# Conditioning tiles of two merges: multiplied and summed on VectorE instead of on TensorE

## The reference: what is computed

```
mc = split(silu(c_ctx) @ w_ada + b_ada, 6)      # context: shift1, scale1, gate1, shift2, scale2, gate2
ml = split(silu(c)     @ w_ada + b_ada, 6)      # latent tokens
merged = sigmoid(g0) * (y_ssd @ w_ssd_out) + sigmoid(g1) * (o_attn @ w_attn_out) + sigmoid(g2) * (o_pool @ w_pool_out)
x = x + gate1 * (merged @ w_out)
x = x + gate2 * moe(rms_norm(x) * (1 + scale2) + shift2)
```

## Time and profile before

| | |
|---|---|
| median of 3 runs | 2200.2 us (2199.82 to 2204.6) |
| the profiled execution | 2198.22 us, its span 2195.4 us |
| TensorE busy | 2054.4 us, 94% |
| VectorE busy | 1247.5 us, 57% |
| ScalarE busy | 956.9 us, 44% |
| DMA | 461.06 MB, 210 GB/s mean |
| conditioning matmuls, whole kernel | 134.4 us busy |

### The profile page before, as it was taken

How to read it: one execution, slowest core, us unless ns; L and a number is a source line. 1 busy time by engine, 2 the same in 40 slices (tenths; PEclk the granted TensorE clock), 3 DMA queues, 4 the chain that set the end, 5 groups by cost and what they waited for, 6 DMA issues and landing times. The chain is left out here.

```text
span 2195.4 us, 28102 instructions
## 1 busy us (share of the span) xinstructions
PE 2054.4 (94%) x11162; PEld 1732.8 (79%) x11162; DVE 1247.5 (57%) x1787; ACT 956.9 (44%) x1372; POOL 7.8 (0%) x12
## 2 busy tenths in 40 slices
PE   7899999989999999999999969987999999999994
PEld 2399988967888899999999958877777777777773
DVE  1467675426554333335433333365779879879996
ACT  1333564322443322223222233343667667667772
POOL 0000000000000000000000000000000000000000
PEclk9999999999999999999999989997999999999997
DMA  9944333333334555553455456532889889899991
GB/s 369 377 125 147 113 123 120 116 132 132 129 129 144 192 191 181 193 214 116 155 192 192 190 185 236 210 116 108 308 307 341 277 306 342 275 307 343 327 365 75
DMA packets 133521, 461.06 MB, mean 210 GB/s; under 512 B 17568, under 2 KB 23520, under 8 KB 133248
## 3 DMA queue, kind: packets, MB, share of 16 engines
q1 hardware_dynamic: 133376, 459.12, 58.8%
HBM read 455.06 MB, written 4.00 MB: 209 GB/s over the span
## 5 line engine op out<-in xcount | busy, mean ns | idle before, releaser
L180 DVE TENSOR_TENSOR wlo<-raw,whi 128x1024 fp32r<-128x1024 f32 x640 | 780.2, 1224 | 752.4 <-ACT whi L174 732.6
L174 ACT ACTIVATE whi<-raw 128x1024 fp32r<-128x1024 f32 x640 | 678.5, 1060 | 900.4 <-PE bank L202 446.3
L200 PE MATMUL bank<-hhi,whi 128*128 128x384 f32 x1664 | 569.0, 342 | 8.8 <-DVE wlo L180 3.6
L202 PE MATMUL bank<-hhi,wlo 128*128 128x384 f32 x1664 | 558.7, 336 | 0.0
L201 PE MATMUL bank<-hlo,whi 128*128 128x384 f32 x1664 | 558.5, 336 | 0.0
L200 PEld LDWEIGHTS bank<-hhi,whi 128*128 128x128 f32 x1664 | 314.0, 189 | 39.1 <-issue 24.1
L201 PEld LDWEIGHTS bank<-hlo,whi 128*128 128x128 f32 x1664 | 314.0, 189 | 0.8
L202 PEld LDWEIGHTS bank<-hhi,wlo 128*128 128x128 f32 x1664 | 313.8, 189 | 0.0
L2062 PE MATMUL bank<-whi,group_hi 128*128 128x512 f32 x512 | 203.1, 397 | 4.9 <-DVE wlo L180 3.7
L2064 PE MATMUL bank<-wlo,group_hi 128*128 128x512 f32 x512 | 201.6, 394 | 0.0
L2063 PE MATMUL bank<-whi,group_lo 128*128 128x512 f32 x512 | 201.0, 393 | 0.0
(11 more groups left out here) (309 smaller groups left out, 1983.9 us busy)
## 6 DMA issues: line engine op xcount, KB each, us to landing
raw<-in_dense SPq DMA_DIRECT2D x448, 512.0 KB, 5.4
raw<-in_moe SPq DMA_DIRECT2D x384, 512.0 KB, 5.0
merged<-in_x SPq DMA_DIRECT2D x8, 768.0 KB, 7.5
cs_rows_bc<-cs_rows SPq DMA_DIRECT2D x8, 768.0 KB, 5.1
out_y<-y_normed SPq DMA_DIRECT2D x3, 768.0 KB, 3.3
shift_rows<-cs_rows SPq DMA_DIRECT2D x2, 1024.0 KB, 9.2
pool_w_sb<-in_pool_w SPq DMA_DIRECT2D x1, 1024.0 KB, 6.9
pool_inv_count<-in_pool_inv SPq DMA_DIRECT2D x1, 768.0 KB, 4.9
```

What stands on the lines that cost most here:

```text
L174: self.nc.scalar.activation(self.whi[:, k % W, :], self.raw[:, n % R, :], ACT.Copy).then_inc(self.hi_done, 1)
L180: self.nc.vector.tensor_tensor(self.wlo[:, k % W, :], self.raw[:, n % R, :], self.whi[:, k % W, :].bitcast(F32), ALU.subtract).then_inc(se ...
L200: self.nc.tensor.matmul(out, self.whi[:, s, c], xhi[:, k, :], start=(k == 0), stop=False)
L202: last = self.nc.tensor.matmul(out, self.wlo[:, s, c], xhi[:, k, :], start=False, stop=(k == blocks - 1))
```

## The change

In the second and third merge TensorE no longer multiplies the conditioning tiles. VectorE does, from the same buffers in `raw`: for each half tile of 512 columns and for each of the two vectors one operation `parts` = `raw` x scalar + `parts` (a TENSOR_SCALAR without the addition for the first half tile of a chunk), the scalar being one value per partition from `cond_padded`. These are 4 operations a tile and 32 a chunk. In each turn 2 stand at A, 3 at B and 3 at C, behind the split and the merge there (`PART_STEPS`). The buffer of a conditioning tile is released when its four operations have ended (`load` waits for `s_part`, named `cond_part_added`). `parts` is double, by chunk. TensorE adds the sums over the partitions with 8 matmuls of one column a chunk, with `parts` as weights (`part_fold`). The copy of rows on ScalarE goes. The first stage, the first merge and the output projection are as before.

```diff
--- before.py
+++ after.py
@@ -103,6 +103,8 @@
         self.dve_steps = Steps(None, nc.alloc_semaphore("dve_steps"))
         self.used = nc.alloc_semaphore("tile_used")
         self.ada_used = nc.alloc_semaphore("cond_tile_used")
+        self.s_part = nc.alloc_semaphore("cond_part_added")
+        self.by_dve = 0
         self.tile0 = 0
         ada_ssd, merge, qkv = ADA_FIRST * ADA_BODY + 2 * SSD_BLOCKS, len(MERGE_ORDER) * 4, 2 * ATT_BLOCKS
         self.order = [ADA_BODY * c + t for c in ADA_START for t in range(ADA_BODY)] + list(range(ADA_FIRST * ADA_BODY, ada_ssd)) + list(range(ada_ssd + merge, ada_ssd + merge + qkv)) \
@@ -154,8 +156,11 @@
 
     def load(self, sp, n):
 
-        if n - R in self.cond_no:
-            sp.wait_ge(self.ada_used, self.cond_no[n - R] + 1)
+        k = self.cond_no.get(n - R)
+        if k is not None and PART_TILES[0] <= k < PART_TILES[1]:
+            sp.wait_ge(self.s_part, 4 * (k - PART_TILES[0] + 1))
+        elif k is not None:
+            sp.wait_ge(self.ada_used, k + 1 - (PART_TILES[1] - PART_TILES[0] if k >= PART_TILES[1] else 0))
         elif n >= R:
             sp.wait_ge(self.lo_done, self.own(n - R) + 1)
         src = self.io.dense[self.order[n]] if n < self.dense_tiles else self.io.moe[(n - self.dense_tiles) % self.moe_tiles]
@@ -221,6 +226,9 @@
 
 MERGE_ORDER = among(12, "ooaao" * 4)
 OUT_ORDER = among(8, "aaoo" * 4)
+PART_CHUNKS = (ADA_FIRST + 4, ADA_FIRST + 12)
+PART_TILES = (PART_CHUNKS[0] * ADA_BODY, PART_CHUNKS[1] * ADA_BODY)
+PART_STEPS = (2, 3, 3)
 MERGE_ADA_END = MERGE_ORDER.index(("ada", ADA_BODY - 1))
 
 
@@ -233,10 +241,39 @@
     last.then_inc(N.ada_used, 1)
 
 
+def part_add(N, eng, ops, i, body, n):
+
+    a, kk, g = n // 4, n // 2 % 2, n % 2
+    p, k = i + N.ada0, 2 * a + kk
+    done = 32 * (p - PART_CHUNKS[0]) + n
+    tile = N.tile(i, body, MERGE_ORDER.index(("ada", a)))
+    if n % 4 == 0:
+        N.wait_landed(eng, tile)
+    w, c, out = N.raw[:, tile % R, kk * 512:kk * 512 + 512], N.cst[:, k, g:g + 1], N.parts[:, p % N.parts.shape[1], g, :]
+    if k == 0:
+        ops.tensor_scalar(out, w, c, None, ALU.mult).then_inc(N.s_part, 1)
+    else:
+        eng.wait_ge(N.s_part, done - 1)
+        ops.scalar_tensor_tensor(out=out, in0=w, scalar=c, in1=out, op0=ALU.mult, op1=ALU.add).then_inc(N.s_part, 1)
+
+
+def part_fold(N, pe, p):
+
+    _s_row, s_fold, s_add = N.ada_sems
+    pe.wait_ge(N.s_part, 32 * (p - PART_CHUNKS[0] + 1))
+    pe.wait_ge(s_add, p)
+    for q in range(4):
+        for g in range(2):
+            last = N.nc.tensor.matmul(N.bank[6][:, 2 * q + g:2 * q + g + 1], N.parts[:, p % N.parts.shape[1], g, q * P:q * P + P],
+                                      N.ones[:, 0:1], start=True, stop=True)
+    last.then_inc(s_fold, 1)
+    N.folded = p + 1
+
+
 def cond_fold(N, pe, p):
 
     s_row, s_fold, s_add = N.ada_sems
-    pe.wait_ge(s_row, p + 1)
+    pe.wait_ge(s_row, p + 1 - N.by_dve)
     if p:
         pe.wait_ge(s_add, p)
     for q in range(4):
@@ -259,13 +296,13 @@
     n = N.tile(i, body, t)
     N.wait_landed(pe, n)
     if a == 0:
-        pe.wait_ge(N.ada_sems[0], i + N.ada0)
+        pe.wait_ge(N.ada_sems[0], i + N.ada0 - N.by_dve)
     cond_blocks(N, n, a, N.bank[7])
 
 
 def ada_row(N, act, i):
 
-    act.wait_ge(N.ada_used, (i + N.ada0 + 1) * ADA_BODY)
+    act.wait_ge(N.ada_used, (i + N.ada0 + 1 - N.by_dve) * ADA_BODY)
     N.nc.scalar.activation(N.ada_rows[:, :], N.bank[7][:, :], ACT.Copy).then_inc(N.ada_sems[0], 1)
 
 
@@ -972,7 +1009,7 @@
     nc.all_engine_barrier()
 
 
-def merge_phase(N, ohi, olo, first, name, side=None, lead=0):
+def merge_phase(N, ohi, olo, first, name, side=None, lead=0, parts=None):
 
     nc, body = N.nc, len(MERGE_ORDER)
     N.tile0 += lead
@@ -995,6 +1032,12 @@
         @block.gpsimd
         def _(pool):
             side.pool(pool)
+            if parts == "pool":
+                for i in range(iters):
+                    if i:
+                        pool.wait_ge(N.ada_sems[1], N.ada0 + i)
+                    for n in range(4 * ADA_BODY):
+                        part_add(N, pool, nc.gpsimd, i, body, n)
 
         @block.scalar
         def _(act):
@@ -1013,7 +1056,7 @@
                     act.wait_ge(N.out_read, N.m0 + m + 1)
                     act.wait_ge(N.used, N.own(N.tile(i, body, t)))
                     nc.scalar.activation(gt[:, :], gate_bank, ACT.Tanh, scale=0.5).then_inc(N.gate_read, 1)
-                if t == MERGE_ADA_END + 1:
+                if t == MERGE_ADA_END + 1 and not parts:
                     ada_row(N, act, i)
                 for _ in range(side.steps(12 * i + o)):
                     next(beside, None)
@@ -1051,6 +1094,10 @@
                     next(beside, None)
                 if o == 1 and i > 0:
                     ada_add(N, dve, i - 1)
+                if parts == "dve":
+                    at = 8 * (o // 3) + sum(PART_STEPS[:o % 3])
+                    for n in range(at, at + PART_STEPS[o % 3]):
+                        part_add(N, dve, nc.vector, i, body, n)
             merge(*before)
             ada_add(N, dve, iters - 1)
             for _ in beside:
@@ -1060,13 +1107,19 @@
         def _(pe):
             beside = side.pe(pe)
 
+            def fold(i):
+                if not parts:
+                    ada_fold(N, pe, i)
+                else:
+                    part_fold(N, pe, i + N.ada0)
+
             def middle(i, o):
 
                 if side.steps(12 * i + o) == 2:
                     next(beside, None)
                 if o == 1 and i > 0:
                     side.fold_free(pe)
-                    ada_fold(N, pe, i - 1)
+                    fold(i - 1)
                 yield
 
             for s in range(lead):
@@ -1076,7 +1129,8 @@
                 next(beside, None)
             for i, t, kind, o in slots:
                 if kind == "ada":
-                    ada_product(N, pe, i, body, t, o)
+                    if not parts:
+                        ada_product(N, pe, i, body, t, o)
                     continue
                 m = i * 4 + o // 3
                 if lead and m == 0 and o % 3 != 1:
@@ -1092,9 +1146,10 @@
                 next(beside, None)
             for _ in beside:
                 pass
-            ada_fold(N, pe, iters - 1)
+            fold(iters - 1)
     N.tile0 += iters * body
     N.ada0 += iters
+    N.by_dve += iters if parts else 0
     N.m0 += KB
     N.blk0 += lead // 2
 
@@ -1819,7 +1874,7 @@
                     last.then_inc(s_sum, 1)
             pe.wait_ge(s_gb, 1)
             pe.wait_ge(s_ld, 80)
-            pe.wait_ge(N.ada_sems[0], N.ada0 + iters)
+            pe.wait_ge(N.ada_sems[0], N.ada0 + iters - N.by_dve)
             for c in range(NCH):
                 for b in range(c + 1):
                     mm(B[7][:, c * NG:(c + 1) * NG], (E.tri if b == c else N.ones)[:, :], E.gb[:, b, :], start=(b == 0), stop=(b == c))
@@ -2143,9 +2198,11 @@
     N = Net(nc, io)
     mix_phase(N)
     merge_phase(N, N.S["hi"], N.S["lo"], True, "ssd", Attention(N))
-    merge_phase(N, N.S["hi"], N.S["lo"], False, "attn", HeadsSplit(N))
+    heads = HeadsSplit(N)
+    N.parts = N.keep_top("cond_parts", [P, 2, 2, 512], F32)
+    merge_phase(N, N.S["hi"], N.S["lo"], False, "attn", heads, parts="dve")
     pooling = Pooling(N)
-    merge_phase(N, N.S["hi"], N.S["lo"], False, "pool", pooling, 2 * POOL_BLOCKS)
+    merge_phase(N, N.S["hi"], N.S["lo"], False, "pool", pooling, 2 * POOL_BLOCKS, parts="dve")
     N.at = N.arena
     split_merged_phase(N)
     E = Experts(N)
```

## The result

The changed kernel takes 2236.6 us, the median of 4 runs (2233.9 to 2241.9), against 2200.3 (2199.8 to 2204.6, 4 runs) before: a ratio of 1.016 with a 95% interval of 1.014 to 1.019. The forecast was 2224, between 2208 and 2248. The direction, the range and the loop that the forecast described held. The loss is 36 us, where the forecast's terms gave 25.

What follows compares the result with a forecast made beforehand. TensorE's instruction stream was taken to bound the kernel, and the change to close a longer loop through VectorE. Stage terms +11.2 and +14.0 us sum to +25.2 on 2198.2, 2223.4, given as 2224 with the median's offset; range 2208 to 2248.

Steps and rivals of the forecast that it cites:

- the loop: In the merges, a1's release, C's load and split, then VectorE's operations form a loop: 14.75 us a turn, before 13.94.
- Spacing of the operations: New VectorE operations in the merges start 0.66 us apart, bounds 0.60 and 0.75.
- Rival 2: Waits on their own semaphore keep VectorE's new operations from overlapping: 8 x 0.09 us more a turn, +22, 2246 us; 15%.
- The load: In the merges, C's load, now first of its burst, lands 3.6 us after issue, bounds 3.4 and 4.0.
- Rival 4: C lands late in the merges, as a second load did (4.8 us): 36 us more, 2260; 5%.
- Rival 1: The loop does not bind and TensorE stays the limit, at a turn of 12.45 us: 2165 us; 9%, partial gains included.
- The signs that it named: Second merge, if right: C every 14.7 us, TensorE some 85% busy at clock 1.00, its idle times ending by `wlo`.
- End of the second merge: Last release at 982.4, then fold and bias addition 2.0 us, to 984.4: +11.2 us.
- End of the third merge: Ends at 1289.7 with fold and bias addition at 2.0 us: +14.0 us.
- The extra wait for a0's buffer: Before the third merge's last split, VectorE waits 4.2 us once more for the tile going into that buffer.
- What follows keeps its length: Pooling tiles and the split of the merged sum, behind a barrier, keep their length: nothing added.
- rival 5: TensorE idles in the merges and its clock falls to 0.83: unhindered turn 15.0 us, kernel 2231; 4%.

Runs made afterwards that it cites:

- experiment 4: Changed kernel with all eight VectorE operations of a turn at A, none at B and C (PART_STEPS 8, 0, 0): 2166.0 us, ratio 0.9839 to the kernel before.
- experiment 5: Changed kernel with only the context vector's operations, 4 a turn instead of 8, at the change's places: 2173.8 us, ratio 0.9870 to the kernel before.
- experiment 6: Changed kernel with TensorE also doing the old conditioning matmuls, sums for these chunks unused: 2234.1 us, ratio 1.015 to the kernel before.
- experiment 7: Changed kernel with the eight operations none at A, four at B, four at C (PART_STEPS 0, 4, 4): 2239.2 us, ratio 1.018 to the kernel before.
- experiment 2: Changed kernel with the eight operations four at A, four at B, none at C (PART_STEPS 4, 4, 0): 2187.5 us, ratio 0.9925 to the kernel before.
- experiment 3: Changed kernel with the eight operations five at A, three at B, none at C (PART_STEPS 5, 3, 0): 2187.3 us, one run.

## Why the prediction was right, and what was too small

- **What bounds the kernel, and the loop.** Right. C's splits lie 14.63, 14.82 and 14.43 us apart (the last with two of the shorter operations). Fourteen turns of the second merge (its first merge operation at 767.8, the 15th at 973.04) take 205.2 us; the forecast has 14 x 14.75 - 1.26 = 205.2.
- **Its terms.** Right within 0.11 us each: release to split 4.65 against 4.76; split, merge and addition 783.59 - 781.27 = 2.32 against 2.32; the rest 791.25 - 783.59 = 7.66 against 7.67. TENSOR_SCALAR took 0.483 us, estimated 0.49.
- **Spacing of the operations.** 0.66 held. Of `[2.07 x3]` the last is 0.75 and the two before it 0.66 each. Rival 2 (no overlap, 2246) fell. The Trainium skill's section "The DRAIN you can't avoid" ("VectorE: DVE Perf Modes"), read as no overlap, would have given 0.75; with 0.66, where each operation waits only for the one before the last, the trace disagrees; by it the time would have been rival 2's.
- **The load.** The first load of a burst landed after 3.5, 3.7 and 3.8 us in three turns; 3.6 was taken. From the Trainium skill ("DMA: Bandwidth & Descriptors", section "Anatomy of one DMA — SWDGE (gpsimd) path"), which is on loads issued by GpSimd, 3.2 us is the estimate for 512 KB. These three loads, issued by SyncE, are 0.3 to 0.6 us above it. Rival 4 (C lands late) fell.
- **Rival 1.** Fell for this order. Experiments 4 and 5 show that it decides where the forecast put it, at a loop of 12.45 us.
- **The signs that it named.** C comes every 14.3 to 15.0 us in the second merge, and the longest waits of the loads are for the new operations, as it said. TensorE was busy 93% in the window from 770 to 965 and not 85%, and its waits end with the merge operation and not with `wlo`. A clock under 1.00 in the merges was named as a sign of being wrong, and it came, at 0.96. It did not change the length of the turn, for the loop does not run over TensorE (experiments 6 and 7).
- **End of the second merge.** Forecast +11.2 us, measured +11.7: the last operation ended at 981.87 instead of 982.4, but the fold and the bias addition took 3.0 us instead of 2.0. The loop's start, the split of B that the forecast had at 759.17, was at 758.76 in this trace, so from there on the loop fits within 0.1 us.
- **End of the third merge.** The fold is the mis-sized term, "16 rows at the 0.1 us that the old 8 imply ... 2.0 us". The fold took 3.57 us and stands in these rows of TensorE, VectorE and the window over them:

```profile
1302.20 3.57 PE L267 MATMUL bank<-ones,cond_parts 128*128 128x1 f32 x16 [8.83 <-DVE cond_parts L257]
```
```profile
1305.88 0.17 DVE L290 TENSOR_TENSOR mods<-bank,b_ada_sb 128x8 f32<-128x8 f32 x1 [2.68 <-PE bank L267]
```
```profile
1302.10:1306.00 3.90, 3.57 (x16) 3.49 (x16) 1.19 (x4) 0.00 (x0) 0.00 (x0) 0.50 0.73 226
```

  TensorE had waited 8.83 us and ran at 0.50, its lower level of 1.2 GHz, where the fold inside a turn, at clock 1.00, took 1.84 us:

```profile
809.74 1.84 PE L267 MATMUL bank<-ones,cond_parts 128*128 128x1 f32 x16
```

  From the last operation (1302.15) to the end of the bias addition (1306.05) it is 3.9 us, 1.9 more than forecast. Some 0.3 of that is no matter of the clock: where the fold ran at nearly full speed (1.95 us, the second merge of experiment 7), the two took 2.27 us. The 17 stage-end folds of all traces with the new operations go with the wait in front of them: 1.84 us without a wait (3 of them); 1.94 or 1.95 (4), 3.13 and 3.57 behind waits of 2.3 to 2.7 us; 2.70, 2.88, 3.57 and 3.58 behind 3.8 to 3.9 us; 3.57 or 3.58 (4) behind over 8 us. From the split at the start of the third merge on, the last operation came 0.7 us later than forecast; together the third merge's own part is +16.7 where +14.0 was forecast. The extra wait for a0's buffer, forecast at 4.2, is there as VectorE's idle time of 4.16 before the split at 1298.93.
- **"What follows keeps its length".** This step failed, by 2.0 us in the profiled pair. The pooling stage began at clock 0.76, where before it was 1.00. The first ten microseconds of before and of after:

```profile
973.20:983.20 10.00, 9.53 (x55) 9.56 (x56) 2.45 (x2) 2.97 (x5) 1.47 (x1) 1.00 0.88 340
```
```profile
984.90:994.90 10.00, 9.52 (x43) 9.55 (x44) 1.24 (x3) 2.12 (x2) 1.46 (x1) 0.76 0.98 373
```

  Twelve matmuls fewer at some 0.17 us are the 2.0 us. From there on the two kernels keep step to 0.01 us: VectorE's last `pool_sums` operation starts at 1048.36 and 1062.08, 75.16 and 77.17 us behind the end of the second merge's last bias addition. The split of B behind it, from which the third merge was counted, has moved by the same 13.72 us, so the two operations in front of pooling's last products cost nothing, as forecast.

  That the change is what slows the start of pooling is not shown. The same ten microseconds in the slower of the two further profiles of the kernel before, and in experiment 5, where TensorE had not waited and its fold had just taken 1.84 us:

```profile
977.30:987.30 10.00, 9.53 (x46) 9.56 (x47) 2.28 (x3) 2.12 (x2) 1.47 (x1) 0.83 0.86 326
```
```profile
956.80:966.80 10.00, 9.50 (x46) 9.53 (x47) 1.26 (x2) 2.12 (x2) 1.46 (x1) 0.83 0.99 379
```

  The stretch to the last `pool_sums` was 75.2, 75.2 and 76.7 us in the three profiles of before, 75.1 in experiment 4, and 76.6 to 78.0 in the eight other profiles with the change or a variant of it. The low start is more frequent with the change, but one of three profiles without it has it too.
- **The clock (rival 5).** It was priced as a fall in every turn. The clock did fall, to 0.96 over the merge, and experiment 6 shows that this costs next to nothing there. It costs where the next step waits for TensorE: the folds at the two stage ends show it. In experiment 4, where TensorE did not wait in front of them, both took 1.84 us. For the start of pooling and the output projection, whose lengths also go with the clock, the traces do not show what lowered it.

The sum: forecast 25.2; plus 0.5 at the end of the second merge, 2.0 in pooling, 2.7 in the third merge, less 0.2 up to `mod_a`, is 30.2, which is what the traces show there. The other 6.5 us of the profiled pair lie behind the merges, where the profiles of before alone differ by 2.3; they are the part that is not explained. A slip of 1.4 us is in the forecast's last step: 2223.4 and the 2.0 us by which the median was higher make 2225.4, not 2224. What was missing in the forecast and is shown is a term for the folds at the stage ends, sized at 2.0 us and measured at 3.0 and 3.9: TensorE had waited, and ran them at a lower clock. The 2.0 us in pooling and the 6.5 us behind the merges were put at nothing; what caused them stays open.

## What to carry to other kernels

When work moves from one engine to another, ask first who then releases the buffer, and which tile the ring puts into that buffer. If the releasing engine's next instruction needs just that tile, the whole load (here 4.65 us with the copy) enters its turn and no busy share shows it; then move as much as possible of what does not need the tile behind the release, as experiments 2 to 4 did with one split and with two. Here the same eight operations cost 36 us, or gained 34, by whether the last of them stood behind or in front of two splits. When the bound moves off TensorE, add a term for a low clock in what it does right behind a long wait if something else waits for that: here 3.57 us for a fold that took 1.84 without a wait.

## What the runs showed of the hardware

TensorE's clock fell inside a stage in which it was almost always busy. In this window of the changed kernel it was busy throughout, 15.00 of 15 us, behind a wait of 1.88 us, and the mean was 0.89; in the timeline matmuls over 384 columns stood 0.32 us apart for 3.2 us, and 0.17 us at the full clock:

```profile
798.00:813.00 15.00, 15.00 (x85) 15.00 (x84) 10.10 (x14) 3.00 (x4) 0.00 (x0) 0.89 0.52 173
```
```profile
798.64 0.52 PE L207 MATMUL bank<-ssd_out_hi,wlo 128*128 128x384 f32 x1
798.96 0.52 PE L205 MATMUL bank<-ssd_out_hi,whi 128*128 128x384 f32 x1
...
802.10 0.34 PE L206 MATMUL bank<-ssd_out_lo,whi 128*128 128x384 f32 x1
```

TensorE waited up to 2.0 us in front of C, 13.8 us in 12 waits over the second merge. With the conditioning matmuls back in the same turns (experiment 6) the mean over the merge was 1.00. Waits alone do not tell, though: experiment 7 had turns as long and TensorE idle for 17.8 of 195 us, more than the 13.1 of the changed kernel, and its mean there was 0.99.

On VectorE, operations of 0.75 us over 128 x 512 that add into two sums in turn, so that each waits for the one before the last, started 0.66 us apart. Where each waited for the one right before it, they started 0.85 us apart (experiment 5).
